# A two-block transformer kernel on one core: fewer filler products, an earlier query row and a later load of constants in the opening

## The chip, the cores and the metric

The kernel runs on one core of a Trainium2 chip. The metric is the device time of one execution in microseconds (us). Each kernel is run several times and the median is given. One further execution is taken by the hardware profiler; the rows of this text come from it.

## What is computed

Two blocks run one after the other on a 512 x 1024 activation x. Only the first layer of the first block matters for this change; everything is float32.

```python
def layer(x, ctx, c, c_ctx, w_mod, b_mod, g_pre, ...):
    shift, scale, gate = jnp.split(jax.nn.silu(c) @ w_mod + b_mod, 3, axis=-1)
    shift_c, scale_c, gate_c = jnp.split(jax.nn.silu(c_ctx) @ w_mod + b_mod, 3, axis=-1)
    hx = rmsnorm(x, g_pre) * (1 + scale[:, None]) + shift[:, None]
    hc = rmsnorm(ctx, g_pre) * (1 + scale_c) + shift_c
    q, k, v, ga, uf, gf, zc, bc, cc, gc = split_cols(hx @ w_in, PROJ_SIZES)
    ...  # the same projections of hc, attention, a Fourier mix, a short convolution
    x_new = x + gate[:, None] * rmsnorm(y, g_post)
```

So two condition vectors are multiplied by the 1024 x 3072 matrix w_mod; its first two thirds (shift and scale) must be known before the normalised rows of x (512) and of ctx (256) can go into the projections. The second layer, and the second block with its two layers (attention of three kinds and a gated feed-forward part), follow and are not touched.

## The kernel before

**Precision.** A product that counts is made of three: each operand is split into a rounded part (hi) and the rest (lo), and `mm3` (L1444 to L1446) adds hi x lo, lo x hi and hi x hi in PSUM. For a weight tile of 128 x 2048 the hi part is made by ScalarE in two halves of 1024 columns (L874), the lo part by GpSimd in four pieces of 512 columns (L800). The hi parts of the activation rows are made by ScalarE (L965 for x, L959 for ctx), the lo parts by VectorE for x (L2189) and by GpSimd for ctx (L807).

**The stream of tiles.** All weights come in as tiles of 1 MB, in the order of the list `stream`, through three buffers `raw` (RAW is 3), issued by SyncE. Tile n goes into the buffer of tile n - 3, so SyncE first waits until that one was used. The stream opens with the eight tiles of w_mod for shift and scale, in the order FIRST (columns 0, 4, 1, 5, 2, 6, 3, 7 in units of 256); then come the second query tile (0,"q",1), the two halves WEIGHED[0] and WEIGHED[1] of a gate tile of w_mod, the key and value tile (0,"kv"), two more gate tiles, and (0,"uf"). The first query tile Q0 has a buffer of its own (`q0_raw`), is issued behind the second tile of FIRST, and ctx (`res_c`) behind the fourth.

**The opening on TensorE**, by hand, in program order:
- `warm(n)` issues n products of 128 x 128 ones; each shows as two matmuls in the trace (L1550). Nothing reads their result. 14 and 10 of them stand ahead of the first tile.
- `first_mod(i)` (L1568) multiplies the two condition vectors by tile i of FIRST: 16 matmuls. ScalarE copies the row out (`first_row`, L954), `first_turn(i)` (L1576) turns it into columns, VectorE adds the bias (`first_in`, L2320), and behind each odd tile makes the scale (L2327).
- `turn_x(0, k)` (L1589) transposes chunk k of the normalised x; VectorE scales and shifts it (L2337), ScalarE and VectorE split it. `turn_ctx` (L1601) is the same for ctx, with ScalarE for the scaling (L986).
- `q0_x(k)` adds chunk k of x into the first query projection: two column halves with `mm3`, six matmuls of 512 columns. It waits for the lo part of chunk k and for the piece of Q0's lo part that holds chunk k (a piece of 512 columns holds two chunks). `q0_ctx(k)` does it for ctx.

**VectorE behind the opening.** After the last rows of x it runs `weigh(0)` and `weigh(1)`: WEIGHED[0] and WEIGHED[1] times the condition, 2 TENSOR_SCALAR (L2267) and 14 SCALAR_TENSOR_TENSOR (L2270) of 128 x 512. Their sum is first read by TensorE in the projection (0,"kv",1).

**SyncE and the constants.** In the loop over the stream, just ahead of the load of WEIGHED[0], SyncE waits until Q0's lo part is complete and issues eight loads `consts` (tables of cosine and sine, masks, sink, small tables; L735), two of the Fourier matrices (L737), and four of w_fourier (L741), some 1.4 MB together. TensorE waits for `consts` behind (0,"q",1), at L1738, and for the Fourier constants behind (0,"kv"), at L1755; VectorE waits for `consts` behind `weigh(1)`.

Of the kernel before, what the change touches and what calls it, by code (L numbers as in the profile page):

```python
# [23 lines left out]
SEQ, CTX, DEPTH = 512, 256, 2  # L24
# [3 lines left out]
HD = 64  # L28
# [106 lines left out]
def _program(nc, I, out, seen):  # L135
    ctx = ExitStack()
    with ctx:
# [11 lines left out]
        def put(name, shape, dt=F32):  # L149
            nonlocal off  # L150
            t = at(name, shape, off, dt)
            off += -(-4 * int(np.prod(shape[1:])) // 32) * 32
            return t
# [46 lines left out]
        dft_ccos = put("dft_ccos", [P, P])  # L200
        dft_csin = put("dft_csin", [P, P])
        wf = put("wf", [P, DEPTH, 2, P])
# [105 lines left out]
        s_consts = Signal(nc, ctx, seen, "consts")  # L308
# [78 lines left out]
        s_tile_lo = Signal(nc, ctx, seen, "tile_lo")  # L387
# [10 lines left out]
        s_wf_landed = Signal(nc, ctx, seen, "wf_landed")  # L398
        s_wf_m = Signal(nc, ctx, seen, "wf_m")
        s_wf_mm = Signal(nc, ctx, seen, "wf_mm")  # L400
        s_wf_zero = Signal(nc, ctx, seen, "wf_zero")
# [87 lines left out]
        WEIGHED = [(l, "mod", jb, kh) for l, jb in BLOCKS for kh in range(2)]  # L489
# [10 lines left out]
        Q0 = (0, "q", 0)  # L500
# [38 lines left out]
        def wait_landed(eng, what):  # L539
            if what == Q0:  # L540
# [5 lines left out]
        consts = [(cos1[:], I["cos1"]), (sin1[:], I["sin1"]),  # L546
                  (band_mid[:], I["band_mid"]), (band_first[:], I["band_first"]),
                  (sinks[:], I["sink"].rearrange("l h -> (l h)").partition_broadcast(P)),
                  (table[0:BUCKETS, :], I["rel_bias_2"]), (table[BUCKETS:, :], I["pick"]), (hot[:], I["hot"])]
# [131 lines left out]
        def bank_of(y, what, t):  # L681
            if what == "h":
                return 2 * (t % 2)
            return 2 * ((t + 2) % 4) if y == DEPTH else 2 * t
# [21 lines left out]
        @block.sync  # L706
        def _(sp):

            def load_rows(i):

                t = 2 * i
                sp.dma_start(res[:, t:t + 2, :], I["x"][0, t * P:(t + 2) * P, :].rearrange("(t p) d -> p t d", p=P)).then_inc(s_x_landed[i].sem, 16)

            for n, (what, loads, _) in enumerate(stream):
                if what[1:] == ("zc",):
                    sp.wait_ge(s_proj.sem, s_proj.at((what[0], ("kv",), 0, 0)))
                    for part, a, e in ((0, 0, 2), (1, 2, 5)):
                        for to in range(0, P, 16):
                            own = to ^ 16
                            sp.dma_start(swap[part][to:to + 16, :, :], qk[own:own + 16, a:e, 0:SEQ]).then_inc(s_swapped[part].sem, s_swapped[part].nth(what[0], 16))  # L720
                if n >= RAW:
                    if stream[n - RAW][0] in FIRST:
                        sp.wait_ge(s_mm.sem, s_mm.at(("tile", stream[n - RAW][0])))
                    elif stream[n - RAW][0] in WEIGHED:
                        sp.wait_ge(s_weigh.sem, s_weigh.at(stream[n - RAW][0]))
                    else:
                        sp.wait_ge(s_tile_lo.sem, s_tile_lo.at(stream[n - RAW][0]))
                if n == 0:
                    load_rows(0)
                    for dst, src in vectors[4:9]:  # L730
                        sp.dma_start(dst, src).then_inc(s_vectors.sem, 16)
                if what == WEIGHED[0]:
                    sp.wait_ge(s_tile_lo.sem, s_tile_lo.at(Q0))
                    for dst, src in consts:
                        sp.dma_start(dst, src).then_inc(s_consts.sem, 16)  # L735
                    for dst, src in ((dft_ccos[:], I["dft_ccos"]), (dft_csin[:], I["dft_csin"])):
                        sp.dma_start(dst, src).then_inc(s_wf_landed.sem, 16)  # L737
                    sp.wait_ge(s_wf_zero.sem, s_wf_zero.at(0))
                    for l in range(DEPTH):
                        for h in range(2):  # L740
                            sp.dma_start(wf[HD * h:HD * h + HD, l, :, HD * h:HD * h + HD],  # L741
                                         I["w_fourier"][l].rearrange("(c h) a b -> h a c b", h=2)[h]).then_inc(s_wf_landed.sem, 16)
                if what == (0, "out", 0, 0):
                    sp.wait_ge(s_bias_row.sem, 16)
                    for h in range(A_HEADS + B_HEADS):
                        sp.dma_start(scratch[h].rearrange("(p n) -> p n", n=SEQ + P),
                                     row[h:h + 1, :].broadcast_to((P, SEQ + P))).then_inc(s_bias_rows.sem, 16)
                if what[1:] == ("out", 1, 0):
                    l = what[0]
                    sp.wait_ge(s_gate_vec.sem, s_gate_vec.at(l))  # L750
                    for s in range(2 - l):
                        sp.dma_start(gate_rows[l, s].rearrange("(c p) -> p c", p=P), mod_g[:, s, :], allow_slow_non_contiguous=True).then_inc(s_gate_row.sem, s_gate_row.nth(l, 16))
                if what in ((1, "q", 0), (DEPTH, "c", 0)):
                    l = what[0] - 1
                    sp.wait_ge(s_gate_row.sem, s_gate_row.at(l))
                    sp.wait_ge(s_lo.sem, s_lo.at((l, "s", SIDES[3])))
                    sp.wait_ge(s_scores.sem, s_scores.at((l, len(units1(l)) - 1)))
                    for s in range(2 - l):
                        sp.dma_start(gate_b[:, s, :], gate_rows[l, s].partition_broadcast(P)).then_inc(s_gate_b[s].sem, s_gate_b[s].nth(l, 16))
                if what == (DEPTH, "c", 0):  # L760
                    sp.wait_ge(s_row_stored.sem, s_row_stored.at(7))
                    sp.dma_start(rot[:], I["rot"]).then_inc(s_rot_in.sem, s_rot_in.nth(0, 16))
                if what == (1, "q", 1):
                    sp.wait_ge(s_scores.sem, s_scores.at((0, len(units1(0)) - 1)))
                    for dst, src in ((cos1[:], I["cos1"]), (sin1[:], I["sin1"])):
                        sp.dma_start(dst, src).then_inc(s_cos_again.sem, s_cos_again.nth(1, 16))
                for into, src in loads:
                    sp.dma_start(into(raw[:, n % RAW, :]), src).then_inc(landed_sems[n % RAW], 16)  # L768
                if n == 0:
                    for dst, src in vectors[9:14]:  # L770
                        sp.dma_start(dst, src).then_inc(s_vectors.sem, 16)
                    load_rows(1)
                if n == 1:
                    for into, src in q0_loads:
                        sp.dma_start(into(q0_raw[:]), src).then_inc(s_q0_landed.sem, 16)
                if n == 3:
                    sp.dma_start(res_c[:], I["ctx"][0].rearrange("(t p) d -> p t d", p=P)).then_inc(s_x_landed[2].sem, 16)
            for t in range(XT - 1):
                sp.wait_ge(s_x_final.sem, s_x_final.at((2 * DEPTH - 1, t)))
                sp.dma_start(out[0, P * t:P * t + P, :], res[:, t, :]).then_inc(s_stored.sem, 16)  # L780
            for half in range(2):
                a = 512 * half
                sp.wait_ge(s_x_final.sem, s_x_final.at((2 * DEPTH - 1, XT - 1, half)))
                sp.dma_start(out[0, P * (XT - 1):P * XT, a:a + 512], res[:, XT - 1, a:a + 512]).then_inc(s_stored.sem, 16)
            sp.wait_ge(s_stored.sem, 16 * (XT + 1))
# [634 lines left out]
        def _(pe):  # L1420
# [126 lines left out]
            def warm(n):  # L1547

                for _ in range(n):
                    pe.matmul(ps[:, 3, 0:P], ones[:], ones[:], start=True, stop=True)  # L1550
# [77 lines left out]
            def q0_x(k):  # L1628

                q0_rows(0, k, (0,))  # L1630
# [7 lines left out]
            pe.transpose(ps[:, 2, 0:NV], vec[0:NV, :], ident[0:NV, 0:NV]).then_inc(s_vec_mm.sem, s_vec_mm.nth(1))  # L1638
            emptied[2] = s_vec_t.after(1)
            first_turn(0)  # L1640
            warm(12)
            first_mod(1)
            first_turn(1)
            turn_x(0, 0)
            turn_x(0, 1)
            warm(4)
            first_mod(2)
            q0_x(0)
            first_turn(2)
            first_mod(3)  # L1650
            turn_x(0, 2)
            turn_x(0, 3)
            first_turn(3)
            q0_x(1)
            first_mod(4)
            q0_x(2)
            first_turn(4)
# [24 lines left out]
            for l in range(DEPTH):  # L1682
# [76 lines left out]
                for g in range(nt // 2):  # L1759
                    b = (7, 6, 5)[g]  # L1760
# [130 lines left out]
            for l in range(DEPTH):  # L1891
# [13 lines left out]
                for t, kh in ((0, 0), (1, 0), (0, 1), (1, 1), (2, 0), (2, 1), (3, 0), (3, 1)):  # L1905
                    if len(ws) == kh:
                        ws.append(both_parts(begin((y, "c", kh)), lambda r: r[:, 0:4 * 416].rearrange("p (k c) -> p k c", k=4)))
                    b = bank_of(y, "t", t)
# [101 lines left out]
                for c in range(3):  # L2010
                    b = CB["kn"][c]
# [11 lines left out]
                for t in range(XT):  # L2023
                    b = VCB[t]
# [31 lines left out]
                for step in range(FROM, STEPS):  # L2056
# [3 lines left out]
                    if r is not None:  # L2060
                        i, b = RANKS[r], TURNED["unit", r]
# [71 lines left out]
                for j in range(2, FC):  # L2133
                    w = begin((y, "ff", j))
                    b = 2 * ((j + 2) % 4)
# [705 lines left out]
```

## Time and profile before

| | us |
|---|---|
| median of 3 runs | 1905.51 |
| lowest, highest of the 3 | 1905.31, 1907.5 |
| the profiled execution, its own time | 1906.53 |
| its span, first to last instruction | 1904.30 |
| outside the span | 2.23 |

The span holds 26728 instructions. TensorE is busy in nearly all of it; the other engines in 37 to 43%. All times below are counted from the start of the span. PE is TensorE's matmuls, DVE VectorE, ACT ScalarE, POOL GpSimd, SPq SyncE's queue of instructions. Matmuls are pipelined: one row's end overlaps the next row's start, so the pace is read from start to start.

### The profile page before, as it was taken

What the parts mean: (1) busy time and instruction counts of PE and PEld (TensorE: products, weight loads), DVE (VectorE), ACT (ScalarE), POOL (GpSimd) and SP (SyncE); (2) the same over time, 40 slices, a digit from 0 to 9 for tenths busy, and PEclk for the clock granted to TensorE, in tenths of its full rate; (3) what the DMA queues carried; (4) which work ended last, traced back from release to release, by engine and by line L of the source; (5) the groups of instructions that cost most, each with busy time, mean ns of one, the idle gap of its engine ahead of it and who ended that gap; (6) DMA issues with size and microseconds to landing.
All of it is one profiled execution on the core that took longest, in us unless ns stands there. A gap on an engine that the chain in (4) does not pass through costs nothing.

```text
span 1904.3 us, 26728 instructions
## 1 busy us (share of the span) xinstructions
PE 1873.8 (98%) x10356; PEld 1604.3 (84%) x10356; DVE 792.5 (42%) x1801; ACT 822.3 (43%) x1577; POOL 713.8 (37%) x567
## 2 busy tenths in 40 slices
PE   8999999999999999999999999999999999999997
PEld 7888899878889888888988888888888898888886
DVE  4584575267455363775311110057277541111003
ACT  5222386382276474873322222127487332232212
POOL 2433221245422444203544544444420345444452
PEclk9999999999999999999999999999999999999999
DMA  9554411125311233202333333223320332332321
GB/s 322 197 150 146 142 23 67 56 67 162 131 23 54 85 96 106 82 2 89 89 91 109 89 102 120 91 88 98 116 84 1 89 89 88 105 94 89 133 89 44
DMA packets 198316, 185.62 MB, mean 97 GB/s; under 512 B 27246, under 2 KB 165636, under 8 KB 198192
## 3 DMA queue, kind: packets, MB, share of 16 engines
q1 hardware_dynamic: 183640, 172.52, 28.9%
q10 hardware_dynamic: 14552, 11.40, 2.2%
q8 instruction: 84, 1.38, 0.3%
q14 instruction: 40, 0.33, 0.1%
HBM read 179.11 MB, written 5.44 MB: 97 GB/s over the span
## 4 chain that ended last, share of the span: by engine, by line
PE 89%; ACT 3%; DVE 2%; issue 2%; POOL 2%; SPq 1%; DMA 1%; DVEq 0%; ACTq 0%
PE ps L1444 25%; PE ps L1446 24%; PE ps L1445 24%; PE ps L2051 3%; PE ps L1537 3%; PE ps L1967 3%; PE ps L2069 2%; PE ps L1504 2%; PE ps L1523 2%; POOL w_lo L800 2%; PE ps L1465 1%; ACT w_hi L874 1%; DMA raw<-in_w_mod 1%; SPq L768 0%; ACT pt L935 0%
## 5 line engine op out<-in xcount | busy, mean ns | idle before, releaser
L800 POOL TENSOR_TENSOR w_lo<-raw,w_hi 128x512 fp32r<-128x512 f32 (+1 forms) x505 | 667.8, 1353 | 1074.5 <-ACT w_hi L874 1074.4
L874 ACT ACTIVATE w_hi<-raw 128x1024 fp32r<-128x1024 f32 (+3 forms) x255 | 252.1, 1034 | 247.2 <-PE ps L1446 190.9
L1444 PE MATMUL ps<-g_hi,w_lo 128*128 128x512 f32 (+1 forms) x928 | 348.4, 375 | 1.4 <-POOL w_lo L800 1.4
L1445 PE MATMUL ps<-g_lo,w_hi 128*128 128x512 f32 (+1 forms) x928 | 347.4, 374 | 0.0
L1446 PE MATMUL ps<-g_hi,w_hi 128*128 128x512 f32 (+1 forms) x928 | 347.4, 374 | 0.0
L1444 PEld LDWEIGHTS ps<-g_hi,w_lo 128*128 128x128 f32 x928 | 174.7, 188 | 34.0 <-issue 1.7
L1445 PEld LDWEIGHTS ps<-g_lo,w_hi 128*128 128x128 f32 x928 | 174.7, 188 | 31.0
L1446 PEld LDWEIGHTS ps<-g_hi,w_hi 128*128 128x128 f32 x928 | 174.7, 188 | 30.9
L2796 DVE TENSOR_TENSOR tmp_f<-ps,tmp_f 128x512 f32<-128x512 f32 x44 | 30.4, 692 | 370.3 <-PE ps L1446 370.3
L1444 PE MATMUL ps<-h_hi,w_lo 128*128 128x512 f32 (+1 forms) x496 | 177.1, 357 | 2.3 <-DVE h_lo L2189 2.3
L1445 PE MATMUL ps<-h_lo,w_hi 128*128 128x512 f32 (+1 forms) x496 | 174.6, 352 | 0.0
L1446 PE MATMUL ps<-h_hi,w_hi 128*128 128x512 f32 (+1 forms) x496 | 174.5, 352 | 0.0
L1444 PE MATMUL ps<-w_hi,hid_lo 128*128 128x512 f32 x352 | 137.1, 390 | 0.0
L1446 PE MATMUL ps<-w_hi,hid_hi 128*128 128x512 f32 x352 | 136.9, 389 | 0.0
L1445 PE MATMUL ps<-w_lo,hid_hi 128*128 128x512 f32 x352 | 136.9, 389 | 0.0
L1399 ACT ACTIVATE hid_hi<-tmp_f 128x512 fp32r<-128x512 f32 x44 | 27.8, 632 | 237.2 <-DVE tmp_f L2796 237.2
L2754 DVE SCALAR_TENSOR_TENSOR res<-res,ps 128x512 f32<-128x512 f32 x32 | 21.8, 685 | 231.6 <-PE ps L1446 231.3
L1444 PE MATMUL ps<-w_hi,g_lo 128*128 128x512 f32 (+3 forms) x320 | 114.2, 357 | 1.5 <-POOL w_lo L800 1.5
L1446 PE MATMUL ps<-w_hi,g_hi 128*128 128x512 f32 (+3 forms) x320 | 112.0, 350 | 0.0
L1445 PE MATMUL ps<-w_lo,g_hi 128*128 128x512 f32 (+3 forms) x320 | 111.7, 349 | 0.0
L1444 PEld LDWEIGHTS ps<-h_hi,w_lo 128*128 128x128 f32 x496 | 93.8, 189 | 21.0 <-issue 8.7
L1446 PEld LDWEIGHTS ps<-h_hi,w_hi 128*128 128x128 f32 x496 | 93.8, 189 | 12.9
(294 smaller groups left out, 3388.3 us busy)
## 6 DMA issues: line engine op xcount, KB each, us to landing
raw<-in_w_in SPq DMA_DIRECT2D x33, 1024.0 KB, 4.9
raw<-in_w_mod SPq DMA_DIRECT2D x24, 1024.0 KB, 6.5
raw<-in_w_gate SPq DMA_DIRECT2D x44, 512.0 KB, 3.7
raw<-in_w_up SPq DMA_DIRECT2D x44, 512.0 KB, 4.8
raw<-in_w_down SPq DMA_DIRECT2D x22, 1024.0 KB, 4.7
raw<-in_w_out SPq DMA_DIRECT2D x8, 1024.0 KB, 5.3
strips<-bias_rows ACTq DMA_DIRECT2D x18, 256.0 KB, 3.2
raw<-in_w_o SPq DMA_DIRECT2D x4, 1024.0 KB, 4.8
```

The costliest lines, as they stand in the source:

```text
L800: pool.tensor_tensor(w_lo[:, i % SPLIT, a:e], raw_of(what)[:, a:e], w_hi[:, i % SPLIT, a:e].bitcast(F32), ALU.subtract).then_inc(s_tile_lo ...
L874: act.activation(w_hi[:, i % SPLIT, a:b], raw_of(what)[:, a:b], ACT.Copy).then_inc(s_tile_hi.sem, s_tile_hi.nth((what, n)))
L1444: pe.matmul(o, lhs[1], rhs[0], start=first, stop=False)
L1445: pe.matmul(o, lhs[0], rhs[1], start=False, stop=False)
L1446: return pe.matmul(o, lhs[0], rhs[0], start=False, stop=last)
L1504: m = pe.matmul(ps_flat[:, o0 + CTX + col:o0 + CTX + col + k.shape[1]], q, k, start=j == 0, stop=j == len(products) - 1)
L1523: m = pe.transpose(ps_flat[:, o0 + P * j:o0 + P * j + P], s_[:, i % n_b, P * j:P * j + P], ident[:])
L1537: m = pe.matmul(ps_flat[:, o0:o0 + HD], turned, v, start=j == 0, stop=j == n - 1)
L1967: pe.matmul(ps[:, b, 0:u["n"]], u["q"], u["k"], start=True, stop=True).then_inc(s_scores.sem, s_scores.nth((y, i)))
L2051: m = pe.matmul(ps[:, b, 0:HD], pt2[r % N_P][:, P * j:P * j + P], v, start=j == 0, stop=j == len(u["vs"]) - 1)
L2069: m = pe.transpose(ps[:, b, P * j:P * j + P], probs_of(i)[:, P * j:P * j + P], ident[:])
L2796: V.tensor_tensor(tmp_f[:, 2 + j % 2, :], ps[:, 2 * ((j + 2) % 4) + 1, :], tmp_f[:, j % 2, :], ALU.mult).then_inc(s_glu.sem, s_glu.nth((y, ...
```

## The change

Three edits:

1. Of the twelve products on ones between `first_turn(0)` and `first_mod(1)`, seven stay.
2. The four products on ones ahead of `first_mod(2)` go, `q0_x(0)` stands there in their place, and `q0_x(1)` takes the old place of `q0_x(0)`, behind `first_mod(2)`; it no longer stands behind `first_turn(3)`.
3. The 14 loads of constants are issued behind the load of WEIGHED[1] instead of ahead of the load of WEIGHED[0].

```diff
@@ -729,17 +729,6 @@
-                if what == WEIGHED[0]:
-                    sp.wait_ge(s_tile_lo.sem, s_tile_lo.at(Q0))
-                    for dst, src in consts:
-                        sp.dma_start(dst, src).then_inc(s_consts.sem, 16)
-                    for dst, src in ((dft_ccos[:], I["dft_ccos"]), (dft_csin[:], I["dft_csin"])):
-                        sp.dma_start(dst, src).then_inc(s_wf_landed.sem, 16)
-                    sp.wait_ge(s_wf_zero.sem, s_wf_zero.at(0))
-                    for l in range(DEPTH):
-                        for h in range(2):
-                            sp.dma_start(wf[HD * h:HD * h + HD, l, :, HD * h:HD * h + HD],
-                                         I["w_fourier"][l].rearrange("(c h) a b -> h a c b", h=2)[h]).then_inc(s_wf_landed.sem, 16)
@@ -766,6 +755,17 @@
                 for into, src in loads:
                     sp.dma_start(into(raw[:, n % RAW, :]), src).then_inc(landed_sems[n % RAW], 16)
+                if what == WEIGHED[1]:
+                    sp.wait_ge(s_tile_lo.sem, s_tile_lo.at(Q0))
+                    for dst, src in consts:
+                        sp.dma_start(dst, src).then_inc(s_consts.sem, 16)
...
@@ -1638,20 +1638,19 @@
             first_turn(0)
-            warm(12)
+            warm(7)
             first_mod(1)
             first_turn(1)
             turn_x(0, 0)
             turn_x(0, 1)
-            warm(4)
+            q0_x(0)
             first_mod(2)
-            q0_x(0)
+            q0_x(1)
             first_turn(2)
             first_mod(3)
             turn_x(0, 2)
             turn_x(0, 3)
             first_turn(3)
-            q0_x(1)
             first_mod(4)
```

## Rows read from the trace of the kernel before

**Rows 1.** The page's first part: busy us (share of the span), instructions of TensorE.
```profile
PE 1873.8 (98%) x10356; PEld 1604.3 (84%) x10356; DVE 792.5 (42%) x1801; ACT 822.3 (43%) x1577; POOL 713.8 (37%) x567
```
**Rows 2.** TensorE's waits, 40 to 1904 us: us in total, times, longest.
```profile
PE ps L1523 <- ACT pt L935: 4.4, 10, 1.0
```
**Rows 3.** The chain that ended last, 0 to 46 us: start, us, what.
```profile
16.55 2.63 SPq L777
19.23 11.20 DMA raw<-in_w_mod
30.56 1.07 PE ps L1568 x16
```
**Rows 4.** TensorE in order of time, 13 to 31 us: start, us, what [idle before].
```profile
13.41 3.09 PE L1550 MATMUL ps<-ones 128*128 128x128 f32 x14
...
13.41 4.55 PE L1550 MATMUL ps<-ones 128*128 128x128 f32 x24
17.90 1.07 PE L1568 MATMUL ps<-raw,cond_wide 128*32 128x256 f32 x16
...
20.85 1.06 PE L1550 MATMUL ps<-ones 128*128 128x128 f32 x8
22.78 1.07 PE L1568 MATMUL ps<-raw,cond_wide 128*32 128x256 f32 x16 [0.88 <-DMA raw<-in_w_mod]
23.78 0.50 PE L1444 MATMUL ps<-h_hi,w_lo 128*128 128x512 f32 x1
...
30.56 1.07 PE L1568 MATMUL ps<-raw,cond_wide 128*32 128x256 f32 x16 [0.92 <-DMA raw<-in_w_mod]
```
**Rows 5.** DMA issues, 5.2 to 5.7 us: KB, us from issue to landing (issued 5.28).
```profile
raw<-in_w_mod SPq DMA_DIRECT2D x1, 1024.0 KB, 11.1
```
**Rows 6.** Stretches of one or two us: busy by engine, clock, DMA share, GB/s.
```profile
10.00:11.00 1.00, 0.00 (x0) 0.00 (x0) 0.00 (x0) 0.00 (x0) 0.00 (x0) 1.00 1.07 433
...
14.00:15.00 1.00, 1.00 (x6) 1.00 (x6) 0.98 (x2) 0.98 (x3) 0.00 (x0) 0.50 1.08 384
...
22.00:24.00 2.00, 1.22 (x17) 0.71 (x18) 1.95 (x3) 1.82 (x4) 1.03 (x2) 1.00 1.06 420
...
28.00:30.00 2.00, 1.64 (x8) 1.03 (x7) 1.75 (x4) 1.48 (x3) 0.00 (x0) 1.00 1.08 386
```
**Rows 7.** ScalarE, VectorE and GpSimd in order of time, 18.9 to 25 us.
```profile
19.04 0.38 ACT L954 ACTIVATE mod_row<-ps 128x256 f32<-128x256 f32 x1 [1.23 <-PE ps L1568]
...
22.26 1.82 DVE L2189 TENSOR_TENSOR h_lo<-tmp_n,h_hi 128x512 fp32r<-128x512 f32 x2
...
20.44 2.49 POOL L800 TENSOR_TENSOR w_lo<-q_raw,w_hi 128x512 fp32r<-128x512 f32 x2 [18.79 <-ACT w_hi L874]
```
**Rows 8.** SyncE's queue in order of time, 34 to 69 us.
```profile
38.91 0.35 SPq L735 DMA_DIRECT2D cos<-in_cos  x1
...
45.88 1.15 SPq L768 DMA_DIRECT2D raw<-in_w_mod  x2
53.67 0.37 SPq L768 DMA_DIRECT2D raw<-in_w_in  x1
```
**Rows 9.** VectorE, then GpSimd, in order of time, 46 to 64 us.
```profile
51.89 2.04 DVE L2267 TENSOR_SCALAR acc<-raw,cond 128x512 f32<-128x512 f32 x2 [3.62 <-DMA raw<-in_w_mod]
53.85 9.36 DVE L2270 SCALAR_TENSOR_TENSOR acc<-raw,cond,acc 128x512 f32<-128x512 f32 x14
...
47.65 1.22 POOL L807 TENSOR_TENSOR h_lo<-tmp_x,h_hi 128x256 fp32r<-128x256 f32 x1 [0.53 <-ACT h_hi L959]
...
59.81 4.55 POOL L800 TENSOR_TENSOR w_lo<-raw,w_hi 128x512 fp32r<-128x512 f32 x1 [6.17 <-ACT w_hi L874]
```
**Rows 10.** GpSimd and VectorE side by side, 75 to 78 us.
```profile
76.98 1.75 POOL L800 TENSOR_TENSOR w_lo<-raw,w_hi 128x512 fp32r<-128x512 f32 x1
...
75.80 3.48 DVE L2270 SCALAR_TENSOR_TENSOR acc<-raw,cond,acc 128x512 f32<-128x512 f32 x2
```
**Rows 11.** TensorE in order of time, at 52, 55, 72 and 90 us.
```profile
52.04 0.28 PE L1444 MATMUL ps<-h_hi,w_lo 128*128 128x256 f32 x1
...
54.91 0.40 PE L1444 MATMUL ps<-h_hi,w_lo 128*128 128x512 f32 x1
...
71.68 1.02 PE L1738 MATMUL ps<-hot,table 34*10 34x512 f32 x2
...
90.41 0.60 PE L1755 MATMUL ps<-wf,dft_ccos 128*128 128x256 f32 x2
```

More of the change, by code:

```diff
@@ L768, in _ @@
                     sp.dma_start(into(raw[:, n % RAW, :]), src).then_inc(landed_sems[n % RAW], 16)
+                if what == WEIGHED[1]:
+                    sp.wait_ge(s_tile_lo.sem, s_tile_lo.at(Q0))
+                    for dst, src in consts:
+                        sp.dma_start(dst, src).then_inc(s_consts.sem, 16)
+                    for dst, src in ((dft_ccos[:], I["dft_ccos"]), (dft_csin[:], I["dft_csin"])):
+                        sp.dma_start(dst, src).then_inc(s_wf_landed.sem, 16)
+                    sp.wait_ge(s_wf_zero.sem, s_wf_zero.at(0))
+                    for l in range(DEPTH):
+                        for h in range(2):
+                            sp.dma_start(wf[HD * h:HD * h + HD, l, :, HD * h:HD * h + HD],
+                                         I["w_fourier"][l].rearrange("(c h) a b -> h a c b", h=2)[h]).then_inc(s_wf_landed.sem, 16)
                 if n == 0:
```

## The prediction

> **What bounds the kernel now.** The page comes first: TensorE is busy in 98% of the span [rows 1], so over the whole kernel only its own work, its clock and its few waits count. Behind 40 us its largest group of waits is 4.4 us, in the first layer's attention, far from the change [rows 2]. The opening is the exception. In the chain that ended last, the reader should see that the first 30 us are not TensorE's at all: the chain runs through SyncE's issues and one transfer. The load of ctx occupies SyncE until 19.18; the fifth tile of w_mod is issued at 19.23 and lands 11.20 us later, at 30.43; `first_mod(4)` starts at 30.56 [rows 3]. The order of TensorE's instructions in time shows the same from its side: it stood idle 0.92 us ahead of that product, and 0.88 us ahead of `first_mod(2)` [rows 4]. The stretches show why nothing comes earlier: from 10 to 32 us the DMA engines move 380 to 430 GB/s with a busy share at or above 1 [rows 6]. The opening up to 30.43 is bound by the transfers, and behind it by TensorE's own list.
>
> **Edit 1, seven products in place of twelve.** The second tile was issued at 5.28 and landed 11.1 us later, at 16.4 [rows 5], but its product started at 17.90, behind the last product on ones [rows 4]. The first 14 matmuls (seven products) run from 13.41 to 16.50 [rows 4], so `first_mod(1)` will start at about 16.5, 1.4 us earlier. It starts at the half clock, which lasts to about 17.1, so it ends near 17.85 in place of 18.97: 1.1 us gained. ScalarE, which had waited 1.23 us for it [rows 7], has its own copy of x done at 17.81 and can follow at once. The chain behind it (row, turn, bias, scale, transposes, shift, hi and lo of chunk 0) comes 1.1 us earlier too: the lo part of chunk 0, in the trace 22.26 to 22.95, will be there at about 21.9. Q0 landed at 19.1, so its first hi half can begin 0.2 us earlier, and GpSimd's first lo piece (20.44 plus half of 2.49 us [rows 7]) is ready by 21.6.
>
> **Edit 2, `q0_x(0)` for four products.** The four products took 20.85 to 21.9 [rows 4] and kept nobody waiting. Now TensorE ends `turn_x(0, 1)` at about 19.8 and waits for chunk 0 until 21.9. From there to the wait for the fifth tile its list is: `q0_x(0)`, `first_mod(2)`, `q0_x(1)`, `first_turn(2)`, `first_mod(3)`, two `turn_x`, `first_turn(3)`. These are the same instructions as between 22.78 and the idle time ahead of 30.56 in the trace, in another order: 30.56 - 0.92 - 22.78 = 6.86 us [rows 4]. The third tile lands at 22.65, before `q0_x(0)` is over (21.9 + 1.5 = 23.4), and the fourth at 25.3, before 26.2, so no transfer stops it. TensorE is through at 21.9 + 6.86 = 28.8 and then waits for the fifth tile, which still lands at 30.43. **The gain ahead of it, 0.9 us, becomes idle time: 0.92 us of waiting turns into about 1.8.** Behind 30.56 the list is the same as before, because `q0_x(1)` was ahead of that wait already. The third tile's buffer is freed 0.5 us later (24.4 in place of 23.85), but its next load then stands behind 6 us of queued transfers, so its landing does not move. Sum of edits 1 and 2 at full clock: 0.
>
> **The clock.** What this leaves open is TensorE's clock. In the trace it fell to half (1.2 in place of 2.4 GHz) at 13.7 us, after an idle time of 1.6 us (10 to 11 us has no TensorE work at all [rows 6]) and a broken stretch behind it. It stayed there to 17.1, and the 24 matmuls on ones took 4.55 us where at full clock, at the 0.11 us a piece of the 8 at 20.85, they take 2.8 [rows 4, 6]: 1.7 us lost. Stretches with idle times of 0.88 and 0.92 us kept the full clock [rows 6]. Now there will be idle times of 2.1 us (19.8 to 21.9) and 1.8 us (28.8 to 30.5), both longer than the 1.6 that stood before the fall. A fall behind the first is paid out of the second: 1.7 of its 1.8 us, cost 0. Two such stretches in a row would cost 2 x 1.7 - 1.8 = 1.6 us, less what the later buffers give back. A fall behind the second idle time lies on work that nothing covers: 1.7 us. So the clock costs between 0 and 1.7 us; a gain is excluded, since from 18 us on the clock was full. I take 0.7, a little under the middle, as one of the two ways is free.
>
> [...]
>
> **Edit 3, constants behind WEIGHED[1].** SyncE passed the wait for the seventh tile at 38.91 and spent until 45.88 on 14 loads; then came WEIGHED[0] and WEIGHED[1] [rows 8]. Now WEIGHED[0] is issued at 38.9 and lands by 44.8 even with the 5.9 us that it took before. WEIGHED[1] waits for the eighth tile's product (41.4) and lands by 48. The constants follow from 42 and are all issued by 49, ahead of the next wait of SyncE's own, which ended at 53.67 [rows 8]. Nothing that stood behind them on the queue is late. TensorE needs the first group at 71.68 and the second at 90.41 [rows 11], over 15 us of cover. What moves is VectorE: it waited 3.62 us for WEIGHED[0], to 51.89 [rows 9], and will start `weigh(0)` at 48.3. Nobody waits for its end: TensorE reads the sum at about 87.
>
> But in 48.3 to 51.9 GpSimd makes the lo parts of ctx chunks 4 to 7 (from 47.65) and then two pieces of the second query tile. Where the two engines' two-input operations meet, the trace shows them blocking each other. Side by side they alternate, each GpSimd piece and each VectorE operation taking 1.75 us in place of about 1.3 and 0.7 [rows 10], a pair in 1.7. I take this case, since GpSimd is there first: its operation is already pending since 47.65. Then chunk 4 is ready at 48.9 as before, chunks 5 to 7 at about 50.0, 51.1 and 52.4 (0.7 us each and one VectorE operation of 0.4 to 0.7 between), the two pieces at 54.1 and 55.8. TensorE reads chunk 4 at 52.04 and chunk 7 at 52.04 + 3 x 0.72 = 54.2, the pieces from 57.7, four products of 0.7 us behind 54.91 [rows 11]. All are in time by 1.8 us or more. The (0,"kv") tile, which waits for the last piece, is issued 2.1 us later. But its first lo piece in the trace was blocked 3.3 us by VectorE to 63.2 anyway (59.81, 4.55 us long [rows 9]); VectorE ends at about the same time now, so the lo part is complete at about 68.5 in place of 68.1, and TensorE wants it at 72.9. Cost 0.
>
> **The sum.** 0 (edits 1 and 2) + 0.7 (clock) + 0 (edit 3) = +0.7 us. On the profiled execution that is 1906.53 + 0.7 = 1907.2; the median stands 1.02 us lower, so I predict 1905.51 + 0.7 = 1906.2.
>
> **Rival A, GpSimd is locked out (slower).** The 4.55 us row shows that a GpSimd operation that arrives while VectorE streams SCALAR_TENSOR_TENSOR gets nothing until the stream ends [rows 9]. If VectorE gets in first at 48.3, two short operations and 14 of 0.67 us (9.36 us [rows 9]) hold GpSimd until 58.4; chunk 4 is ready at 59.1, and TensorE, due at 52.04, stands 7.1 us. With one fall of the clock behind that idle time it is 8.8: 1912.6 to 1914.3. It decides at one point, who has the turn at 48.3. For it speaks that row; against it, that GpSimd is pending first, and that at 51.89 and 75.80 GpSimd kept its turn.
>
> By the Trainium skill (SBUF — State Buffer, section on the two sides) the lock is held for one whole instruction and goes to whoever starts first. GpSimd would then never wait longer than one operation of 0.7 us, and rival A could not happen (1906.2 stands). The 4.55 us row is against that rule.
>
> **Rival B, the fifth tile is not bound by the transfers.** SyncE ended the ctx issue at 19.18, and the tile's buffer came free at 18.97, nearly together. If the buffer was the cause, the tile comes earlier by up to the 1.1 us of edit 1, and so does all behind it: 1904.4. Against it: the ctx issue took 2.63 us, the pace at which 1 MB drains at 386 GB/s, so SyncE was held by a full queue.
>
> **Rival C, no clock cost.** The idle times leave the clock alone, or are paid in full: 1905.5.
>
> **Chances.** Forecast with a clock cost of 0.3 to 1.7 us: 0.50. Rival C: 0.28. Rival A: 0.12. Rival B: 0.06. Anything else, by more than 3.8 us: 0.04. A measurement of this kernel tells about 0.2%, 3.8 us, from no change. Forecast, B and C are all within it: 0.84 together; A gives slower by 7 to 9 us; of the rest 0.01 goes to slower and 0.03 to faster, which makes 0.13 and 0.03. The range 1904.0 to 1909.0 takes in the forecast, B and C (0.84), with the 2 us by which the runs of before differ on the upper side; leaving A out leaves out less than 2 in 10.
>
> **What would show it.** `first_mod(1)` at 16.5 and `q0_x(0)` at 21.9; `first_mod(4)` again at 30.5 to 30.6, behind about 1.8 us of idle time; the clock at 1.00 or 0.50 in 20 to 34 us; VectorE's L2267 near 48.3; the ctx lo parts of chunks 5 to 7 stretched to over 1 us and no idle time of TensorE at 52. The prediction is wrong if `first_mod(4)` starts before 30, or if a GpSimd row of over 5 us stands at 48.

## The result: slower by 0.22%

Over 20 executions each, the changed kernel has a median of 1910.88 us (1906.56 to 1913.06) and the kernel before 1905.75 us (1905.00 to 1907.61). The ratio is 1.0022 with a 95% interval of 1.0016 to 1.0028; it goes with the means, which are 4.1 us apart. The medians are 5.1 us apart (a ratio of 1.0027), the fastest executions 1.6. The time predicted was 1906.2 us, in a range of 1904.0 to 1909.0, "slower" with a chance of 0.13. The profiled execution took 1910.90 us.

The executions of the changed kernel lie in groups: one at 1906.6, seven from 1908.1 to 1908.9, nine from 1910.5 to 1911.5, three at 1913.0. That is itself a reading: something comes in steps of about 2 us. The mean granted clock of each execution goes with them: 0.997 for the five fastest, 0.995 or 0.996 for the twelve behind them, 0.993 for the three at 1913.0. A fall like that in [rows 4], which lost 1.7 us, lowers the mean over 1905 us by 0.0009.

The page's span, and TensorE's clock in 40 slices, where the first slice now shows 8 in place of 9:

```profile
span 1908.6 us, 26691 instructions
...
PEclk8999999999999999999999999999999999999999
```

The chain that ended last, 15 to 46 us (start, us, what), against [rows 3]:

```profile
5.79 13.14 DMA q_raw<-in_w_in
18.96 1.06 ACT w_hi L874
...
20.09 1.28 POOL w_lo L800
21.38 0.64 issue
22.02 0.76 PE ps L1444
...
31.19 0.36 PE ps L1576 x4
31.57 0.18 DVE mod L2319
...
33.55 0.70 DVE h_lo L2188
...
34.39 0.62 PE ps L1444
```

The fifth tile is gone from it. From `q0_x(0)` on the chain stays on TensorE, and leaves it once more, for chunk 2 of x, ahead of `q0_x(2)` at 34.39. Its first part must be read with care. It puts the wait of `q0_x(0)` down to GpSimd's lo part of the query tile, but that piece was done at 21.38, and 0.64 us of "issue" follow for which the chain has no reason. The other thing that `q0_x(0)` waits for is VectorE's lo part of chunk 0:

```profile
20.74 2.85 DVE L2188 TENSOR_TENSOR h_lo<-tmp_n,h_hi 128x512 fp32r<-128x512 f32 x2
```

The first of these two runs from 20.74 to 21.91, and `q0_x(0)` starts 0.11 us later. In five other traces (e0, e3, e4, e6, e11, see below) the start also lies 0.10 us behind the end of that operation. So TensorE waited for chunk 0, as the prediction has it. The operation took 1.17 us here because GpSimd was at work on the query tile: it took 0.69 us in e0, where it began as GpSimd went from one piece to the next, and 1.73 us in e11, where it began behind the start of a piece.

TensorE in order of time, 13 to 45 us (start, us, what [idle before]), against [rows 4]:

```profile
13.24 1.81 PE L1550 MATMUL ps<-ones 128*128 128x128 f32 x14
16.37 1.07 PE L1568 MATMUL ps<-raw,cond_wide 128*32 128x256 f32 x16 [1.32 <-DMA raw<-in_w_mod]
...
22.02 0.76 PE L1444 MATMUL ps<-h_hi,w_lo 128*128 128x512 f32 x1 [2.52 <-POOL w_lo L800]
24.84 1.94 PE L1568 MATMUL ps<-raw,cond_wide 128*32 128x256 f32 x16
...
31.03 0.51 PE L1576 MATMUL ps<-fold,mod_row 128*128 128x2 f32 x4
31.46 1.07 PE L1568 MATMUL ps<-raw,cond_wide 128*32 128x256 f32 x16
34.39 0.62 PE L1444 MATMUL ps<-h_hi,w_lo 128*128 128x512 f32 x1 [1.85 <-DVE h_lo L2188]
...
44.70 1.07 PE L1568 MATMUL ps<-raw,cond_wide 128*32 128x256 f32 x16
```

And stretches of 1 and 2 us (TensorE's busy time comes first behind the comma, its clock third from the end), against [rows 6]:

```profile
14.00:15.00 1.00, 1.00 (x10) 0.86 (x8) 0.94 (x3) 0.98 (x3) 0.00 (x0) 1.00 1.09 386
...
19.00:21.00 2.00, 0.49 (x5) 0.25 (x3) 1.79 (x3) 1.91 (x3) 0.91 (x1) 0.98 1.08 382
21.00:23.00 2.00, 0.98 (x2) 0.83 (x3) 2.00 (x2) 1.31 (x2) 2.00 (x2) 0.50 1.10 403
23.00:25.00 2.00, 2.00 (x9) 1.15 (x11) 0.60 (x1) 0.00 (x0) 2.00 (x3) 0.50 1.02 407
25.00:27.00 2.00, 2.00 (x17) 0.73 (x14) 0.00 (x0) 0.15 (x1) 0.95 (x1) 0.50 1.07 387
27.00:29.00 2.00, 2.00 (x10) 1.63 (x9) 0.00 (x0) 0.23 (x1) 0.00 (x0) 0.82 0.83 246
...
33.00:35.00 2.00, 0.61 (x2) 0.54 (x3) 1.88 (x3) 1.91 (x3) 0.00 (x0) 0.89 1.09 386
35.00:37.00 2.00, 2.00 (x7) 1.51 (x6) 1.39 (x4) 0.68 (x4) 0.00 (x0) 0.50 1.08 386
37.00:39.00 2.00, 2.00 (x22) 1.33 (x21) 0.53 (x2) 0.04 (x1) 0.00 (x0) 0.76 0.19 61
```

The loss of this execution can be read off. `q0_x(0)` waits 2.52 us; the clock is at its lower level (1.2 GHz) from 20.9, still in that wait, to 27.7, and the third tile's product takes 1.94 us in place of 1.07. From `q0_x(0)` to `first_mod(4)` it is 9.4 us (22.02 to 31.46) for the list that the prediction put at 6.86, so the low clock costs 2.6 us here. The fifth tile was issued at 19.06 and landed 10.7 us later, at 29.8; its product starts at 31.46 and waits for nothing, where before it started at 30.56: **0.9 us late**. Behind it TensorE waits 1.85 us for chunk 2, where it had not waited before. Behind that wait the clock is low again, for 0.11 x 2 + 0.50 x 2 + 0.24 x 2 = **1.7 us** of lost clock. 0.9 + 1.85 + 1.7 = 4.5; measured at the eighth tile's product it is 44.70 - 40.38 = 4.3 us (from `q0_x(2)` to that product it is 10.31 us against 8.82, so the last part is 1.5), and the span is 4.3 us longer (1908.6 against 1904.3). Little behind it adds or gives back: behind 45 us no group of TensorE's waits differs from that of before by more than 0.2 us in total.

### The profile page after: what moved, and what is told of

It reads as the page before. It is cut to its first block, busy times and chain, and to the rows that moved or that the text cites. A ratio compares the mean times of both kernels' runs of the same rounds, so it can differ in the third digit from the quotient of the medians.

```text
span 1908.6 us, 26691 instructions
## 1 busy us (share of the span) xinstructions
PE 1873.1 (98%) x10338; PEld 1601.7 (84%) x10338; DVE 795.9 (42%) x1801; ACT 822.0 (43%) x1577; POOL 712.0 (37%) x567
## 4 chain that ended last, share of the span: by engine, by line
PE 90%; ACT 3%; DVE 3%; issue 2%; POOL 2%; DMA 1%; SPq 0%; DVEq 0%; ACTq 0%
PE ps L1444 25%; PE ps L1446 24%; PE ps L1445 24%; PE ps L2050 3%; PE ps L1537 3%; PE ps L1966 3%; PE ps L2068 2%; POOL w_lo L800 2%; PE ps L1504 2%; PE ps L1523 2%; DMA q_raw<-in_w_in 1%; PE ps L1465 1%; ACT w_hi L874 1%; ACT pt L935 0%; DVE y L2564 0%
```

## Experiments

Each kernel is timed beside the kernel before on the same chip, 11 executions against 33. "Theory T" throughout: TensorE comes to `q0_x(0)` too early, idles, its clock falls, and the list behind it is late. The loads land at moments that differ by over 1 us from one trace to another, counted from the start of the span (the fifth tile's product, where it waits for its tile, starts at 30.56 before, at 29.47 in e1, at 28.91 in e4), so between traces waits and distances are compared, not starts.

### One edit at a time

**Edit 3 alone** (`e1_consts_later`): the changed kernel with TensorE's program of before, so that of the change only the move of the 14 loads is left.

> The kernel before with edit 3 alone: the 14 loads of constants behind WEIGHED[1], all 24 products on ones and the old order of the query rows. Theory T (the loss comes from the late first query row and the fall of TensorE's clock behind it, and from chunk 2's chain without cover): edit 3 costs nothing, 1905.2 to 1906.0, with VectorE's L2267 near 48.3 and no idle time of TensorE at 52. Rival R3 (the collisions of VectorE and GpSimd from 48 us on carry the loss): 1908 to 1911.

Measured: 1905.17 us against 1905.35, ratio 1.0000 (0.9991 to 1.0009). VectorE's `weigh(0)` follows its lo parts without a gap (start, us, what):

```profile
45.28 1.93 DVE L2189 TENSOR_TENSOR h_lo<-tmp_n,h_hi 128x512 fp32r<-128x512 f32 x2 [0.84 <-ACT h_hi L965]
47.14 1.84 DVE L2267 TENSOR_SCALAR acc<-raw,cond 128x512 f32<-128x512 f32 x2
```

R3 falls: VectorE no longer waits 3.62 us for WEIGHED[0], and that changes nothing that can be measured.

**Edit 1 alone** (`e2_seven`).

```diff
-            warm(12)
+            warm(7)
```

> The kernel before with edit 1 alone: 7 of 12 products, the rest as before. Theory T: first_mod(1) at 16.5, transposes done by 19.8, the four products then leave 1.7 us of idle time ahead of first_mod(2) at 22.7; a fall of the clock there can cost up to 3.4 us on the list to first_mod(4), less 0.9 of its wait; the second query row still covers chunk 2's chain. 1905.5 to 1908.0, so at most half of the loss. Rival R1 (edit 1 is the whole loss, the missing filler lowers the clock whatever the order): 1909 to 1911.

Measured: 1905.06 against 1905.35, ratio 0.9999 (0.9990 to 1.0007), all 11 executions between 1904.9 and 1905.6. It is less than theory T allowed for. The profiled execution idles 1.39 us ahead of `first_mod(2)` and has the full clock throughout. The time alone would not show that for the others, since the wait for the fifth tile (1.31 us) could hide much of a fall; but the mean granted clock is 0.998 or 0.999 in ten of the 11 executions; in the kernel before it is 0.9981 on average. R1 falls too.

**Edit 2 alone** (`e3_order`).

```diff
             turn_x(0, 1)
-            warm(4)
+            q0_x(0)
             first_mod(2)
-            q0_x(0)
+            q0_x(1)
...
             first_turn(3)
-            q0_x(1)
             first_mod(4)
```

> The kernel before with edit 2 alone: 12 products, q0_x(0) ahead of first_mod(2), q0_x(1) behind it, no four products. Theory T: q0_x(0) waits about 2 us for chunk 0 at about 23, the clock falls behind that idle time, first_mod(4) is 1 to 2 us late and chunk 2's chain is uncovered: 1908.5 to 1912. Rival R1 (edit 1 is the loss): 1905.5 to 1906.5.

Measured: 1908.42 against 1905.35, 3.1 us more, ratio 1.0015 (1.0006 to 1.0024), at the lower edge of what theory T gave. The new order alone makes a loss of this size. Whether edit 1 has a share in the whole is not measured: the changed kernel itself was not timed on this chip, and on the others it lost 5.1, 4.3 and 2.2 us.

### Filler in the idle time

**Ten products ahead of `q0_x(0)`** (`e4_fill_first_gap`), the changed kernel otherwise.

```diff
             turn_x(0, 1)
+            warm(10)
             q0_x(0)
             first_mod(2)
```

> The changed kernel with ten products on ones (20 matmuls, 2.2 us at full clock) ahead of q0_x(0), in the idle time of 2.5 us in which it waits for chunk 0. They add no work that anybody waits for. Theory T: the clock stays at 2.4 GHz in 20 to 28 us, first_mod(4) at 30.5 again, 1905.5 to 1907.2 (the upper end if the clock falls behind the idle time ahead of first_mod(4)). Rival R2 (the order alone costs it, without the clock: late turns and an uncovered chain): 1908.5 to 1911, as the changed kernel.

Measured: 1905.98 against 1905.35, 0.6 us more, ratio 1.0004 (0.9995 to 1.0013). TensorE in order of time:

```profile
17.79 2.40 PE L1550 MATMUL ps<-ones 128*128 128x128 f32 x20
20.51 0.47 PE L1444 MATMUL ps<-h_hi,w_lo 128*128 128x512 f32 x1 [0.33 <-issue]
22.07 1.07 PE L1568 MATMUL ps<-raw,cond_wide 128*32 128x256 f32 x16
...
28.91 1.07 PE L1568 MATMUL ps<-raw,cond_wide 128*32 128x256 f32 x16 [1.48 <-DMA raw<-in_w_mod]
30.27 0.47 PE L1444 MATMUL ps<-h_hi,w_lo 128*128 128x512 f32 x1 [0.30 <-DVE h_lo L2189]
```

The same order with twenty matmuls that compute nothing: the clock is full throughout, TensorE waits for the fifth tile again, as the prediction had it (1.48 us), and 0.30 us for chunk 2. R2, the order by itself, falls as the main cause; 0.30 us of waiting is what is left of it here. The three slowest of the 11 executions (1906.69 to 1907.35) have a mean granted clock of 0.997, the eight others 0.998 or 0.999, so the filler does not seem to shut out every fall.

**Half of the filler, both gaps filled, and the changed kernel again**, on one chip: `e10_fill_half` has `warm(5)` ahead of `q0_x(0)`, `e5_fill_both` has `warm(10)` there and `warm(7)` ahead of `first_mod(4)`, `e11_changed_third` is the changed kernel.

> The changed kernel with five products on ones ahead of q0_x(0): half of the idle time (about 1.3 of 2.5 us) stays. If the clock falls by the length of the idle time: between the changed kernel and the filled one, 0.6 to 1.8 us above before, with fewer executions in the upper groups. If any idle time there brings the fall: as the changed kernel, 2 us and more above.

> The changed kernel with ten products on ones ahead of q0_x(0) and seven ahead of first_mod(4), in the second idle time. Against the kernel with the first ten alone (1905.98 beside 1905.35 of before, three of its executions 1.1 to 2.0 us above the lowest group): if those three are falls of the clock behind the second idle time, they go, and the median is 0.0 to 0.5 us above before; if the rest is only the uncovered chain of chunk 2 (0.3 us of waiting) it stays at 0.3 to 0.6. If the seven products hold first_mod(4) back, it is 0.3 or more worse.

> The changed kernel itself once more, beside the filled ones: 1907 to 1911, 1.5 to 5 us above before. The two measurements so far differ (5.1 and 2.2 us above before), the clock of their executions too; a third says which is usual.

Measured, medians beside 1905.49 of the kernel before: no filler 1909.79 (+4.3, ratio 1.0021, 1.0013 to 1.0030), five products 1906.92 (+1.4, 1.0007, 0.9998 to 1.0015), ten and seven 1906.01 (+0.5, 1.0006, 0.9997 to 1.0015). The step from none to five products is clear: ten of the 11 executions with five are faster than the fastest of the changed kernel (1907.94). The step from five to ten can't be told from none, and neither 1.4 nor 0.5 us can be told from no loss at all. The changed kernel came out as expected. The seven products in the second gap bring nothing beyond the ten: five of the 11 executions still lie between 1906.8 and 1908.5. These five have a mean granted clock of 0.997 and the six others 0.998, which points to falls of the clock; but with that gap filled (0.20 us of idle time left in the profiled execution) the guess that they come from the second idle time is not borne out, and where they fall is in no trace. A fall behind the second idle time does happen. The profiled execution with five products has one (1907.78 us, stretches as above), behind a wait of 1.52 us and the fifth tile's product:

```profile
27.00:29.00 2.00, 0.49 (x6) 0.42 (x5) 1.40 (x4) 0.85 (x3) 0.00 (x0) 1.00 1.09 386
29.00:31.00 2.00, 1.73 (x18) 1.11 (x19) 1.83 (x3) 1.91 (x4) 0.00 (x0) 0.90 1.09 386
31.00:33.00 2.00, 2.00 (x7) 1.53 (x5) 1.44 (x4) 0.63 (x4) 0.00 (x0) 0.50 1.09 387
```

The changed kernel's own profile here, 1912.12 us, has the clock low from 17.1 to 27.3, and again from 34.1 to 37.6:

```profile
17.00:19.00 2.00, 2.00 (x11) 2.00 (x12) 1.01 (x4) 1.06 (x1) 0.00 (x0) 0.52 1.09 387
19.00:21.00 2.00, 0.53 (x3) 0.13 (x1) 2.00 (x3) 1.22 (x3) 1.96 (x2) 0.50 1.09 387
...
25.00:27.00 2.00, 2.00 (x18) 0.71 (x17) 0.00 (x0) 0.00 (x0) 0.06 (x1) 0.50 1.07 379
```

The first fall stands ahead of the wait for chunk 0. The profiles of e0 and of e10 have it at 17 too. What stands in front is the wait for the second tile, 1.4 to 1.5 us in these three, which edit 1 makes: with all twelve products it is 0.3 us (e3's trace):

```profile
14.84 1.07 PE L1568 MATMUL ps<-raw,cond_wide 128*32 128x256 f32 x16 [0.29 <-DMA raw<-in_w_mod]
```

Of the ten traces with seven products three have this fall; of the three experiments with twelve (e1, e3, e8) none has. That is too few to give edit 1 a share in the loss, and enough to leave it open.

### Which part is the clock and which the uncovered chunk

On one chip: `e6_second_row_back` is the changed kernel with `q0_x(1)` back between `first_turn(3)` and `first_mod(4)`, `e7_back_and_fill` the same with `warm(10)` ahead of `q0_x(0)`, `e8_no_four` the kernel before without `warm(4)`, `e0_changed_again` the changed kernel.

```diff
             q0_x(0)
             first_mod(2)
-            q0_x(1)
             first_turn(2)
...
             first_turn(3)
+            q0_x(1)
             first_mod(4)
```

> The changed kernel with q0_x(1) back in its old place, between first_turn(3) and first_mod(4); q0_x(0) stays ahead of first_mod(2), no filler. TensorE waits for chunk 0 as in the changed kernel, so the clock falls as often. Theory T2 (two parts: the fall makes first_mod(4) about 1 us late; the rest is chunk 2's chain, uncovered since q0_x(1) no longer stands between its turn and its first use, and a second fall behind that wait): first_mod(4) again 0.5 to 1.5 us late, but no wait for chunk 2 and no second fall: 1906.0 to 1907.5. Rival R4 (the clock's falls alone, wherever the rows stand): 1908 to 1911, as the changed kernel.

> The same with ten products on ones ahead of q0_x(0). Theory T2: nothing is left of the loss, 1905.0 to 1905.7, and first_mod(4) waits about 1.5 us for its tile. Rival R4: the same. If it stays over 1906.5, the first query row ahead of the third tile costs by itself.

> The kernel before without the four products ahead of first_mod(2); all twelve and the old order of rows stay. TensorE then idles about 2 us ahead of the third tile. Theory T2: a fall of the clock behind that idle time happens in some executions, and what it costs is paid partly out of the wait for the fifth tile; chunk 2 is covered: 1905.2 to 1907.0. Rival R1b (missing filler costs 1.7 us or more for each fall, whatever stands behind): 1907 to 1909.

> The changed kernel itself, unaltered, on this chip beside the others, since the moment at which TensorE's clock falls shifts from execution to execution: 1908 to 1913, median near 1910.5, in groups about 2 us apart (each fall of the clock costs 1.7).

Measured, medians beside 1905.53 of the kernel before:

| kernel | median, us | above before | ratio, 95% interval |
|---|---|---|---|
| e0, the changed kernel | 1907.71 | 2.2 | 1.0012 (1.0003 to 1.0021) |
| e6, second row back | 1907.45 | 1.9 | 1.0010 (1.0002 to 1.0019) |
| e7, second row back, ten products | 1905.47 | -0.1 | 1.0000 (0.9991 to 1.0009) |
| e8, before without its four products | 1906.31 | 0.8 | 1.0003 (0.9994 to 1.0012) |

The changed kernel, e0, was itself expected at 1908 to 1913 and came out lower. e6 lies in its range, but theory T2 had given the move of the second row the larger share, and that is wrong: the move is worth 0.3 us, which this measurement can't tell from none. Rival R4, the clock's falls alone wherever the rows stand, is not excluded: e6 and e0 came out alike. The ten products are worth 2.0 us on top of it, and nothing is left then. The mean granted clock over the 11 executions tells why: 0.9960 in e0, 0.9965 in e6, 0.9981 in e7, and 0.9978 in the kernel before beside them. The move left the falls where they were. A smaller reason is in e6's trace, in an execution with full clock (1906.07 us):

```profile
21.22 0.47 PE L1444 MATMUL ps<-h_hi,w_lo 128*128 128x512 f32 x1 [2.56 <-POOL w_lo L800]
22.75 1.07 PE L1568 MATMUL ps<-raw,cond_wide 128*32 128x256 f32 x16
24.33 0.61 PE L1576 MATMUL ps<-fold,mod_row 128*128 128x2 f32 x4 [0.51 <-ACT mod_row L954]
```

Without a query row between `first_mod(2)` and `first_turn(2)`, the turn waits 0.51 us for ScalarE's copy of the row. The second row covers one of two waits, wherever it stands. e8 lies in T2's range and under R1b's. Without the four products TensorE waits 3.37 us for the third tile, and in the profiled execution its clock falls in that wait, at 20.8:

```profile
21.29 1.94 PE L1568 MATMUL ps<-raw,cond_wide 128*32 128x256 f32 x16 [3.37 <-DMA raw<-in_w_mod]
```

The median is 0.8 us above before, which the interval does not tell from none; the four slowest executions (1906.75 to 1907.84) have a mean granted clock of 0.996 or 0.997, the kernel before 0.998.

**The clock and the time, execution by execution.** For each profiled execution I add up what the clock withheld between 15 and 39 us: for each stretch of 2 us, 2 x (1 - clock). Beside it stands the time of that very execution, less the median of the kernel before on its chip.

| profiled execution | clock withheld, us | above before, us |
|---|---|---|
| e7, e4, e5, e6 | 0 | 0.2, 0.2, 0.3, 0.5 |
| e8, no four | 1.7 | 0.8 |
| e3, order | 1.7 | 1.7 |
| e0, changed | 3.4 | 1.6 |
| e10, five products | 3.4 | 2.3 |
| changed (first measurement) | 5.1 | 5.2 |
| e11, changed | 6.8 | 6.6 |

The withheld clock comes in steps of 1.7 us. Up to 3.4 us, about half to all of it reaches the end. At 5.1 and 6.8 us the loss is as large as the clock withheld, but it is not made of it alone: the wait of 1.85 us for chunk 2 is in it, and part of the low clock fell into waits. Three more traces fit: e1 and e2 (0 us withheld, 0.1 above and 0.4 below before) and the kernel before (1.1 us in this window, 0.8 above its median). One does not: e9, below, has 0 us and lies 1.3 above, for another reason. These are single executions; the order is clear, the exact share is not.

### A try for a faster kernel

`e9_ctx_later`: edits 1 and 3, TensorE's order of before, ctx loaded behind the fifth tile, and

```diff
-            act.wait_ge(s_x_landed[2].sem, 16)
-            squares(0, 4)
             first_rows(1)
+            act.wait_ge(s_x_landed[2].sem, 16)
+            squares(0, 4)
```

> A try for a faster kernel: edits 1 and 3, the old order of rows with the four products, and the load of ctx moved behind the fifth tile of w_mod, with ScalarE's first pass over ctx behind its hi parts of chunks 2 and 3. The fifth tile then lands 2.7 us earlier, and TensorE's wait of 1.3 us for it goes; the sixth tile lands when it did, 0.3 us before TensorE wants it, so it takes back all but 0.3 to 0.5. Expected 0.3 to 0.8 us under before. If ctx comes late for its transposes: no gain, or up to 1 us over.

Measured: 1906.77 against 1905.49, 1.3 us more, ratio 1.0009 (1.0000 to 1.0017), outside what was expected. TensorE's timeline shows where it went:

```profile
28.01 1.07 PE L1568 MATMUL ps<-raw,cond_wide 128*32 128x256 f32 x16
29.43 0.47 PE L1444 MATMUL ps<-h_hi,w_lo 128*128 128x512 f32 x1 [0.35 <-DVE h_lo L2189]
32.21 0.61 PE L1576 MATMUL ps<-fold,mod_row 128*128 128x2 f32 x4 [1.18 <-ACT mod_row L954]
```

The wait for the fifth tile is gone, as meant, but `first_turn(4)` now waits 1.18 us. ScalarE's two passes over ctx (29.18 and 30.24, each 1.05 us long) stand ahead of its copy of that tile's row, which starts at 31.79. The tile came earlier and met a queue that had been laid out for its old time. The three slowest executions (1908.14 to 1909.65) have a mean granted clock of 0.998, which does not point to the clock; what they are is open. No kernel of this study beats the one before by more than its measurement can tell.

## Why the prediction was wrong

**Right.** With the clock held up, TensorE waits for the fifth tile longer than before and nothing is gained: 1.48 us in e4, against 1.8 forecast. Edit 3 costs nothing (e1). In the changed kernel VectorE starts `weigh(0)` as its last lo part ends (at 52.51 in place of the 48.3 forecast, since the list is 4.3 us late), GpSimd's four ctx parts take 4.12 us in place of 3.31, and TensorE has no idle time from 45 to 75 us:

```profile
52.51 1.83 DVE L2266 TENSOR_SCALAR acc<-raw,cond 128x512 f32<-128x512 f32 x2
...
51.97 4.12 POOL L807 TENSOR_TENSOR h_lo<-tmp_x,h_hi 128x256 fp32r<-128x256 f32 x4 [0.53 <-ACT h_hi L959]
56.05 3.44 POOL L800 TENSOR_TENSOR w_lo<-raw,w_hi 128x512 fp32r<-128x512 f32 x2
```

GpSimd, which began 0.54 us ahead of `weigh(0)`, kept its turn; rival A did not happen. Rival B did not happen either. In the changed kernel the fifth tile's buffer came free when `first_mod(1)` ended, at 17.44 in place of 18.97, and SyncE issued the tile at 19.06 in place of 19.23, right behind the load of ctx:

```profile
16.38 2.63 SPq L777 DMA_DIRECT2D res_c<-in_ctx  x1
19.06 13.91 SPq L757 DMA_DIRECT2D raw<-in_w_mod  x4
```

**Right by luck.** `first_mod(1)` at 16.5 (16.37) and `q0_x(0)` at 21.9 (22.02) came out, but not for the reasons given. The forecast had the seven products run at half clock up to 16.50. They ran at full clock, were done at 15.05, and the product waited 1.32 us for its tile, which landed at about the same time. The half clock of [rows 4] stood in an execution 1.0 us above the median and is in none of the three later traces with twelve products (e1, e3, e8); at full clock the twelve still leave 0.3 us of waiting (e3), so edit 1 had nothing to gain. For chunk 0 the prediction read its lo part as 22.26 to 22.95, but the first of the two operations in that row [rows 7] takes 1.22 us and ends at 23.48. It took 0.7 us for the operation, which lasted 1.17, and 1.1 us for the gain ahead of it, where VectorE began 1.5 us earlier; the two errors cancelled.

**Wrong, first: "Behind 30.56 the list is the same as before."** The list of instructions was the same, the cover was not. Between `first_turn(3)` and `q0_x(2)` runs a chain over VectorE and ScalarE (bias, scale, shift, hi, lo of chunk 2), 3.4 us from 31.03 to 34.39 in the changed kernel. A row of before that the prediction does not show has it too: from `first_turn(3)` at 27.64 to the end of VectorE's first lo part at 30.84. Before, `q0_x(1)`, the wait for the fifth tile and its product lay beside it. Now only the wait and the product do, and when the list is late there is no wait. So the 1.8 us of idle time were counted twice in my sum, once as the reserve that pays for a slow clock and once as the cover of this chain. With full clock the chain sticks out by 0.30 us (e4), behind a list that a low clock has made late by 1.2 (e0) to 1.85. This is the smaller of the two errors: covering the chain again without filler (e6) was worth 0.3 us, and most of its size with a late list is the clock's doing.

**Wrong, second, and the step that carries the loss: the clock term, "between 0 and 1.7 us".** Ten products that hold the clock up take back 3.8 of 4.3 us (with seven more, e11 to e5), and all of 1.9 us with the second row in its old place (e6 to e7). The step "two such stretches in a row would cost 1.6 us" was right in kind (0.9 us at the fifth tile, since part of the low clock fell into the wait), but I let each way exclude the others. They add up: the falls behind the first wait use up the reserve, the chain's wait follows, and that wait brings a fall of its own, which nothing covers. The upper end should have been two stretches beyond the reserve, the chain and one more stretch, 1.6 + 1.85 + 1.7 = 5.2 us, from rows that I had, but for the chain's 1.85. Even that is too low: e11 has a third stretch in a row, from 17 on, and the three slowest executions of the first measurement lie 7.3 us above the median of before. The value of 0.7 was mis-sized: the median loss was 5.1, 2.2 and 4.3 us in three measurements.

**By the page.** The Trainium skill (TensorE: Matmul & The Clock Gate, Part 1) says that the clock is at half after idle time and that activity releases it. In direction this case agrees: the changed kernel's clock fell in a wait of 2.52 us, and 2.4 us of products that nobody reads, put into such a wait, took nearly all of the loss (e4, e7). Whether a given wait brings a fall the length of the wait did not decide here: in 2.52 us the clock fell, behind 2.56 us in e6 it stayed full.

## What to carry to other kernels

A wait that is there anyway is one reserve: if it pays for a slower clock it can't also cover a chain. When an instruction is moved, list what ran beside it at its old place, not only what waits for it. Products that nobody reads can hold up the clock: before they are taken out or moved, ask how long the engine is idle in their place, and price a fall there together with what it makes late. And look whether the one profiled execution is a usual one: an edit that mends a fall which only that execution had gains nothing.

## What the runs showed of the hardware

An idle time of the same length does not always bring a fall of the clock. In and behind 2.56 us (e6) it stayed full, in 2.52 us it fell and stayed low for 6.8 us, and in e11 it had fallen already behind 1.36 us and a short run of work. A fall can come inside the wait (e8: it fell at 20.8, the wait ended at 21.3) or after it: in e10 the wait ended at 29.0 and the clock fell at 30.6. So one program has times several us apart on one chip, in steps near 2 us, and a single execution of such a kernel says little. With 1.39 us ahead of `first_mod(2)` (e2) the mean clock was that of before in ten of 11 executions. The changed kernel lost 2.2 us on one chip, 4.3 on another and 5.1 in the first measurement; what makes the difference was not settled.

VectorE's and GpSimd's subtractions, which read two tiles each, hold each other up: the same lo part of chunk 0 took 0.69, 1.17 or 1.73 us (e0, changed, e11), depending on where GpSimd stood.
